# Two-layer streaming encoder: the sample streams as nine units inside the pair pipeline of both attention layers, and the first tile's bias loaded ahead of the band

## The reference, cut to what matters

```
# layer 0: 16 heads in 2 key/value groups; keys = 16 meta + 128 cached + 16 own = 160
keys = concatenate([km, ck, k]);  vals = concatenate([vm, cv, v])
s = einsum(q, keys) * D ** -0.5 + bias          # bias from the distance of query and key
p = sink_softmax(s, sinks)                      # the sink is one more term of the sum
o = einsum(p, vals)
# layer 1: 16 heads, 1 key/value group; keys = 256 cached + 16 own, of which each query
# keeps the 68 with the best index scores, + 16 meta that are always kept = 288
```

## Time and profile before

| | us |
|---|---|
| three runs | 3144.76, 3155.63, 3156.03 |
| median | 3155.63 |
| profiled execution | 3155.8 |
| its span, first to last instruction | 3154.0 |
| stream pipeline and what is ahead of it, layer 0 | 173.5 to 261.2 |
| prompt pipeline, layer 0 | 261.2 to 436.9 |
| stream pipeline, layer 1 | 1740 to 1841 |
| prompt pipeline, layer 1 | 1841 to 2149.3 |

### The profile page before, as it was taken

How to read it: one execution, slowest core, us unless ns; L and a number is a source line. 1 busy time by engine, 2 the same in 40 slices (tenths; PEclk the granted TensorE clock), 3 DMA queues, 4 the chain that set the end, 5 groups by cost and what they waited for, 6 DMA issues and landing times.

```text
span 3154.0 us, 47535 instructions
## 1 busy us (share of the span) xinstructions
PE 2985.0 (95%) x18119; PEld 2784.0 (88%) x18119; DVE 1550.6 (49%) x2822; ACT 708.0 (22%) x1424; POOL 879.8 (28%) x825
## 2 busy tenths in 40 slices
PE   7969999999999999998895999999999999999998
PEld 6957889999999999986585777779899999999997
DVE  5125633644444444454498357552454444444445
ACT  3025631100000000023366236652100000000001
POOL 3212333222222222222033136322322222222221
PEclk9966999999999999999997559999999999999998
DMA  3521001111111111113011100002111111111111
GB/s 116 81 73 33 2 15 41 34 41 40 40 40 40 40 40 40 40 33 116 9 43 39 49 13 2 2 2 83 39 41 40 40 40 40 40 46 41 40 33 70
DMA packets 182948, 130.26 MB, mean 41 GB/s; under 512 B 32241, under 2 KB 172977, under 8 KB 182598
## 3 DMA queue, kind: packets, MB, share of 16 engines
q1 hardware_dynamic: 182818, 128.52, 14.3%
HBM read 112.80 MB, written 15.16 MB: 41 GB/s over the span
## 4 chain that ended last, share of the span: by engine, by line
PE 87%; DVE 6%; issue 4%; SPq 1%; ACT 1%; DMA 0%; DVEq 0%; POOL 0%; POOLq 0%; ACTq 0%
PE ps_gemm L1406 33%; PE ps_gemm L1422 18%; PE ps_gemm L1372 16%; PE ps_tr L1493 4%; PE ps_out L1513 2%; PE ps_tr L1489 2%; PE ps_far L1790 1%; PE ps_far L1623 1%; PE ps_near L1513 1%; PE ps_far L1810 1%; PE ps_out L1510 1%; DVE scm L2340 1%; PE ps_out L1830 1%; PE ps_near L1510 1%; DVE xl L2114 1%
## 5 line engine op out<-in xcount | busy, mean ns | idle before, releaser
L692 DVE TENSOR_TENSOR h<-h,ps_gemm 128x1170 f32<-128x1170 f32 x192 | 263.7, 1374 | 407.4 <-PE ps_gemm L1422 231.8
L1406 PE MATMUL ps_gemm<-xh,w_hi 128*128 128x390 f32 x1920 | 448.1, 341 | 0.0
L1406 PE MATMUL ps_gemm<-xh,w_lo 128*128 128x390 f32 x1920 | 448.1, 342 | 0.0
L1406 PE MATMUL ps_gemm<-xl,w_hi 128*128 128x390 f32 x1920 | 446.0, 340 | 0.0
L1224 POOL CAST w_hi<-w_raw 128x1024 fp32r<-128x1024 f32 x120 | 124.9, 1041 | 1130.9 <-PE ps_gemm L1406 625.6
L1406 PEld LDWEIGHTS ps_gemm<-xh,w_hi 128*128 128x128 f32 x1920 | 352.5, 189 | 0.0
L1406 PEld LDWEIGHTS ps_gemm<-xl,w_hi 128*128 128x128 f32 x1920 | 349.4, 189 | 0.0
L1406 PEld LDWEIGHTS ps_gemm<-xh,w_lo 128*128 128x128 f32 x1920 | 349.1, 189 | 0.0
L1227 POOL TENSOR_TENSOR w_lo<-w_raw,w_hi 128x1024 fp32r<-128x1024 f32 x120 | 287.4, 2395 | 17.4
L1372 PE MATMUL ps_gemm<-xl,w_hi 128*128 128x390 f32 (+1 forms) x1152 | 271.6, 344 | 0.0
L1422 PE MATMUL ps_gemm<-gu_hi,w_hi 128*128 128x390 f32 x1056 | 247.6, 343 | 0.9 <-DVE h L692 0.9
(11 more groups left out here) (378 smaller groups left out, 4609.9 us busy)
## 6 DMA issues: line engine op xcount, KB each, us to landing
w_raw<-in_w_gate SPq DMA_DIRECT2D x44, 512.0 KB, 3.8
w_raw<-in_w_up SPq DMA_DIRECT2D x44, 512.0 KB, 3.8
w_raw<-in_w_down SPq DMA_DIRECT2D x44, 512.0 KB, 3.2
w_raw<-in_w_in_b SPq DMA_DIRECT2D x13, 512.0 KB, 4.0
w_raw<-in_w_qkv_a SPq DMA_DIRECT2D x10, 512.0 KB, 4.0
residual_park<-h SPq DMA_DIRECT2D x1, 4680.0 KB, 13.7
h<-residual_park SPq DMA_DIRECT2D x8, 585.0 KB, 7.5
out<-yt SPq DMA_DIRECT2D x9, 512.0 KB
```

Of the source, the lines that this page charges most:

```text
L692: dve.tensor_tensor(c3(h[:, m, :]), c3(h[:, m, :]), pse(j), ALU.add).then_inc(evac[j % 2], 1)
L1406: mm = pe.matmul(ps[j % 2][:, m_, 0:CH], w[:, k, :], x[:, k, m_ * CH:(m_ + 1) * CH], start=(k == 0 and w is wh and x is XH), stop=(k == KT ...
```

## The change

One list of 73 units, `UNITS`, now serves both layers: the 64 pairs and 9 stream units, of which one follows each sixth pair from pair 11 on (b = -1 is the meta rows, then streams 0 to 7). The pipeline `attention` is gone. A stream unit is both halves of a unit at once: its 128 rows are (head pair, query), its halves r = 0, 1 are the heads of a pair, so all 16 heads go through in one unit. Keys are brought into both halves by products with the identity (`keys_a`, `keys_b`) two steps ahead, and the values' products write the output already transposed. The mask of a stream comes to 128 rows by 8 small DMAs (`mask_s`) and POOL adds it to the bias (`comb_s`). The slots of transposed groups are 4 in both layers. The first tile's bias is loaded first, then `vbd`, then the band; the band's masking is put behind step 4 of the pipeline. In layer 1 the mask steps are two behind each of the first 24 steps. `to_rows` is gone.

```diff
+        UNITS = []
+        for n in range(QT * HEADS // 2):
+            UNITS.append({"n": n, "t": n // 8, "pr": n % 8, "b": None})
+            if n >= 11 and (n - 11) % 6 == 0:
+                UNITS.append({"n": None, "t": None, "pr": None, "b": (n - 11) // 6 - 1})
...
-            if layer == 0:
-                k = j % 6
-                return x12["pta"][:, k, :] if k < 3 else x4["pta_v"][:, k - 3, :] if k < 5 else x4["pta_s"][:]
-            k = (j - NV[1]) % 7
-            return hreg["ptb_a"][:, k, :] if k < 2 else hreg["ptb_b"][:, k - 2, :] if k < 5 else x4["ptb_x"][:, k - 5, :]
+            k = (v - V0[layer]) % 4
+            if layer == 0:
+                return x4["pta_v"][:, k, :] if k < 2 else x12["pta_x"][:] if k == 2 else rreg["pta_r"][:]
+            return hreg["ptb_a"][:, k, :] if k < 2 else hreg["ptb_h"][:] if k == 2 else x4["ptb_x"][:]
...
+            def keys_a(g):
+                j, b = g["j"], UNITS[g["keys"]]["b"]
+                pe.wait_ge(sa_in[b % 2], 48 * (b // 2 + 1))
+                if j >= 2:
+                    pe.wait_ge(p_ev[j % 2], j // 2)
                 for kv in range(KV_A):
+                    d = slice(HD * kv, HD * (kv + 1))
+                    for src, rows, c in ((x12["sa_k"], P, 0), (x12["sa_kc"], 32, P)):
+                        for p in range(2):
+                            mm = pe.matmul(tb[j % 2][HD * p:HD * (p + 1), 160 * kv + c:160 * kv + c + rows],
+                                           src[0:rows, b % 2, d], ident[0:rows, 0:rows], start=True, stop=True)
+                mm.then_inc(p_tr, 1)
...
+            def stream_scores_a(i, b, o):
+                pe.wait_ge(p_q, b + 2)
+                if b >= 0:
+                    j = KEY_GROUP[0][i]["j"]
+                    pe.wait_ge(p_ev[j % 2], j // 2 + 1)
+                for p in range(2):
+                    r = slice(HD * p, HD * (p + 1))
+                    for g in range(KV_A):
+                        c = slice(HD * g, HD * (g + 1))
+                        k = x4["kts_a"][r, g, :] if b >= 0 else kt_a(g)[r, 0:META]
+                        mm = pe.matmul(far[p][c, o:o + unit_width(0, i)], x12["qs_a"][r, c], k, start=True, stop=True)
+                mm.then_inc(p_sc, 1)
...
+                for p in range(2):
+                    r = slice(HD * p, HD * (p + 1))
+                    lhs, x = hreg["qs_b"][r, :], far[p]
...
+                    pe.matmul(x[:, o:o + PAST], lhs, hreg["kts_b"][r, 0:PAST], start=True, stop=True)
+                    pe.matmul(x[:, o + PAST:o + PAST + DEC_SEQ], lhs, x4["kt2"][r, scols(b)], start=True, stop=True)
+                    mm = pe.matmul(x[:, o + 272:o + 288], lhs, hreg["kts_b"][r, PAST:PAST + META], start=True, stop=True)
...
+            def mask_between(n):
+
+                for s in (2 * n, 2 * n + 1):
+                    c, k = divmod(s, MASK_STEPS)
+                    if c < 6:
+                        mask_step(c, k, first_mask + MASK_STEPS * c)
```

More of the change, by code:

```diff
@@ L388, in units_a @@
[L388 to L397, removed]
-                    else:
-                        u["blocks"] = [(1, 32), (33, P)]
-                        u["w"] = 160
-                        if g == 0 and b + 1 < DEC_BATCH:
-                            u["pre"] = [b + 1]
-                    us.append(u)
-            return us
@@ L550, in build, with score_counts @@
+        RED, FREE = reductions()
+        def score_counts():
+            got, count = [[], []], 0
+            for layer in range(2):
+                for i in range(NU):
+                    t = UNITS[i]["t"]
+                    two = layer and t is not None and 3 <= t < 6
+                    got[layer].append((count + 1, count + (2 if two else 1)))
+                    count = got[layer][-1][1]
+            return got
+        SC = score_counts()
         parked = sem("residual_parked")
@@ L1476, in prompt @@
[L1476 removed]
+            def prompt(layer, scores, keys, values, meta_values):
                 def transposes(g):
[L1479 removed]
+                    j, i = g["j"], g["u"]
                     if g["first"]:
[L1481 removed]
+                        pe.wait_ge(p_exp, 2 * (NU * layer + i) + 2)
                     if j >= 2:
                         pe.wait_ge(p_ev[j % 2], j // 2)
[L1484 to L1485 removed]
+                    x = x_of(layer, i)
+                    for k, b in enumerate(g["blocks"]):
@@ L1528, in prompt @@
-                for g in VG[layer][-2:]:
-                    products(g)
+                    gs = AT[layer][n]
+                    if gs and gs[0]["keys"] is not None:
+                        keys(gs[0])
+                        gs = gs[1:]
+                    for k in range(0, len(gs), 2):
+                        for g in gs[k:k + 2]:
+                            transposes(g)
+                        for g in gs[k:k + 2]:
+                            if g["v"] - 2 >= V0[layer]:
+                                products(BY_V[g["v"] - 2])
@@ L1531, in _ @@
+                for v in range(V_END[layer] - 2, V_END[layer]):
+                    products(BY_V[v])
             pe.wait_ge(ident_in, 16)
```

1115 lines of the change are left out of this document (462 added, 653 removed).

## The result

| | before | changed |
|---|---|---|
| median of the runs | 3155.83 us (4 runs) | 3060.4 us (4 runs, 3051.24 to 3061.28) |
| profiled execution | 3155.8 us, span 3154.0 | 3051.24 us, span 3049.5 |
| ratio | 1 | 0.9697, 95% interval 0.9666 to 0.9727 |

The time fell by 95 us by the medians and by 104.5 by the two traces.

The account below looks back on a forecast made before the run. PE was taken to bound the prompt pipelines, with streams costing nearly 190 us at half clock. Layer 0's terms gave -42.6 and layer 1's -56.7, together -99.3 from 3155.8: forecast 3056 us, range 3038 to 3092.

Parts of the forecast that it names:

- Start of layer 0: Layer 0's first prompt reduction at 182.5 in place of 260.45, no stream work ahead: 78.0 us earlier (69 to 80).
- Start of layer 1: Layer 1's first prompt reduction at 1740.3 in place of 1842.42, with the band already landed: 102.1 us earlier (99 to 103).
- The streams: Stream units on PE in both pipelines: 4.0 us per stream, 1.4 for the meta unit, 33.4 us per layer (27 to 46).
- The test named in the prediction: In the pipelines, a gap of about 4.0 us between a stream's scores and those of the next pair.
- The slots: Four slots for transposed groups in place of 6 and 7: costs nothing (0 to +5 us).
- The mask steps: Layer 1, two per step behind the first 24 steps: DVE needs longer than PE in steps 12 to 23, +12 us (0 to +20).
- the sign named for it: In layer 1's steps 12 to 23, PE idle for some 12 us with DVE as releaser.
- The clock: Layer 0's pipeline: the clock could rise later than 23 us after the prompt's start, +2 us (0 to 9).
- Rival A: Low clock in layer 1's steps 12 to 23, perhaps around later streams: +20 to +40 us, 3076 to 3096; chance 0.16.
- B: Both pipelines: each stream unit costs its upper bound, waits adding 1.6 us to each of 16: 3082 us; chance 0.12.
- C: Pipeline starts: layer 0 starts at 191 and layer 1 waits for its band, +9 + 3, 3068 us; chance 0.07.
- D: Both mixed pipelines: the clock never rises, set back by streams and waits on DVE; about 3380 us; chance 0.03.

Follow-up runs that it names:

- the test: Changed kernel plus, at its end, five forms of VectorE mask steps with GpSimd idle, then beside GpSimd's additions; 3144.8 us, 93 us of it these additions to the kernel.
- the control: The changed kernel run again unaltered in a later batch; median 3057.8 us, single runs 3054.6 to 3062.6.
- the trimmed version: Changed kernel with TensorE's idle time ahead of both pipelines filled, by fewer products than in the first fill, and mask steps four per three units; 3029.9 us.
- the best version: The trimmed version with five and three filling products in layer 0 in place of three and one; 3022.0 us, ratio 0.959 to the kernel before.
- the version with both the overrun and the spread steps: Changed kernel with the first, longer fill of TensorE's idle time, which ran past the first reduction in layer 1, and mask steps over 36 units; 3038.7 us.

## Why the prediction was right, and which of its terms were not

The forecast, 3056 us, is 4 us under the median and 5 over the profiled execution, and the mechanism is the one forecast: the streams leave their half-clock stretches, both pipelines start 78 and 105 us earlier, and the streams come back at full clock. That it came within 5 us of the trace owes something to luck. Split by the run without streams, the terms were off by -4.0 (streams, layer 0), +1.7 (clock, layer 0), +1.9 (streams, layer 1), -1.7 (mask steps and clock, layer 1), +0.3 and -3.2 (the two starts) us, which sum to -5. By its own steps:

**Start of layer 0: right.** -78.0 was said, -77.75 measured, with the landing at 181.6 where 182.0 was said.

**Start of layer 1: 3 us short.** -102.1 against -105.3. From the memset to the reduction it was 1.6 us, not 1.9. The rest: the memset itself stood 1297.2 us behind the first product of layer 0's projection, 3.0 less than before. These three lie ahead of the end of layer 1's last projection (1262.4 us behind that product, against 1265.8 before), not in the search. Their cause is open.

**The streams: right in sum, with the wrong split.** 33.4 per layer was said, 66.8 in all; without the streams but with the leading tokens' unit the total fell by 62.7, where 64 would be due. A stream costs 3.5 us in layer 0 and 4.2 in layer 1, not 4.0 in each. The timeline of layer 0 shows the period directly, from the scores of one stream to those of the next; the scores of the next pair follow a stream's after 2.35 us:

```profile
237.20 0.50 PE L1569 MATMUL ps_far<-kts_a,qs_a 64*64 64x160 f32 x8
...
239.55 0.70 PE L1554 MATMUL ps_far<-kt,q 64*128 64x256 f32 x4
...
256.79 0.50 PE L1569 MATMUL ps_far<-kts_a,qs_a 64*64 64x160 f32 x8
```

From stream to stream it is 19.59 us, six pairs of 2.68 and 3.5 for the stream. By starts in the same timeline, these are keys 1.21 us (1.07 was said), scores 0.43 (0.75), transposes 0.59 (0.56), the inverse 0.27 (0.27), values 0.84 (1.06) and 0.17 by which the transposes behind the keys take longer, where 0.3 was put for waiting. The scores and the values were priced too high. The test named in the prediction, a gap of 4.0 us between a stream's scores and the next pair's, was put badly: a stream's work is spread over four steps, and the price is only in the period.

**The slots: nothing speaks against it.** The run with three shows at most some 3 us for a slot less; the step from six and seven to four was not run by itself.

**The mask steps: right in size, and the reason incomplete.** +12 was said; the pipeline of layer 1 without streams is 11.7 us longer than before (with 1.4 for the leading tokens' unit in it), and spreading the steps gives back 11.6. But the sign named for it, PE idle for some 12 us with DVE as releaser, did not come: in the 62 us window PE is idle for 8.1 us, of which 4.2 end with DVE and 3.7 with ACT's copies. The rest goes with the fall of the clock. DVE was taken to be busy with the steps for the time they took before. In fact the same ten groups sum to 46.3 us (1692.3 to 1800) against 39.4, which had one step less. I take GpSimd's additions beside them for the cause. The comparison over 768 elements took 1.73 us in the changed kernel with GpSimd adding, 0.87 in the kernel before, and in the test 0.62 alone and 1.33 beside GpSimd:

```profile
1735.75 1.73 DVE L2324 TENSOR_SCALAR eq<-scm,small 128x768 bf16<-128x768 f32 x1
```

**The clock: wrong reading, small error.** In layer 0 it rose 28.8 us behind the first reduction, not 23, one to two steps late, as allowed for; in the control another 9 us later. Without streams and the leading tokens' unit layer 0's pipeline is 3.7 us longer than before, where +2 stood. Rival A came true in small: the clock did fall once in steps 12 to 23, for 7 us, in the wait on DVE shown above; in the control it fell there for 10 us and again near 1780. What the prediction missed is that in layer 1 it rose after 31.6 us, where before it took 42, which hid that loss.

The Trainium skill, TensorE: Matmul & The Clock Gate, section "What's actually happening", says that TensorE is held at the lower clock by default and that activity releases it. In this case's traces the granted clock stays at 0.50 for 28.8 us in which PE shows as busy for 28.09 (the windows above; the earlier trace rows has the same in the kernel before); with the idle time ahead of the pipeline filled, the same steps run at 1.00. So busy time in the profile alone does not tell which level is granted, and no run here shows what does.

**Profile and median.** By the median the gain is 9 us less than by the trace. The control's trace, at 3054.6 us, has 3.3 us of that in layer 0's pipeline, where the clock rose later. The remainder I put down to the same cause, since the time of single runs falls as their granted clock rises; it is not shown, for only the profiled runs show where the clock is low.

**Rivals.** B (5.6 us a stream) is refuted by the period and by the run without streams, C (191 and a late band) by the first reduction at 182.70 and the band's issue at 1655.93, and D by the clock row. The low end of the range, 3038, was said to be half of the small bounds' 25 us; half would be 3043.5. Nothing here hangs on it.

## What to carry to other kernels

When work at half clock is moved into a pipeline that runs at full clock, price it by the pipeline's own instructions at full clock and check the period over several units; here 4.0 us a stream was said and 3.5 and 4.2 came. Work whose deadline is far off, such as the mask steps, should be paced to its last deadline and not packed into the first steps: one number in the loop gave 12 us. Both pipelines here follow idle time and ran their first steps at half clock; filling that time gave 6 to 10 us in layer 0 and 6 to 8 in layer 1. Fill with as many products as fit and no more, counted from a measured one: with two mask steps per unit, 6 us of gain in layer 1 became 7 us of loss by an overrun.

## What the hardware showed that was not expected

- In these pipelines of short products with many weight loads the clock stayed at 0.50 for 21 to 38 us behind the first reduction though PE shows as busy nearly all the time; once it is up, the same steps mostly keep it at 1.00. It fell at one wait of 2.1 to 2.6 us in each of seven traces, and in the trimmed version behind a wait of 1.83 us; waits of up to 1.1 us in the four traces with spread mask steps left layer 1's pipeline at 1.00.
- The time at which it rises differs by 9 us between two executions of one kernel (28.8 and 37.7 us behind the first reduction). Five runs of the best version, whose trace has no stretch at 0.50 in either pipeline, lie within 1 us; but the five of the version with both the overrun and the spread steps, whose trace has none either, lie 8 us apart, with granted clocks of 0.984 to 0.988.
- A VectorE operation with its inputs in SBUF, beside a GpSimd that adds without a pause, took 0.65 to 0.77 us longer in all five forms tried, whatever its own length (0.62 to 1.76 us); GpSimd's addition took 1.65 us in place of 1.09.
- Three bias loads of 1.2 MB took 6.8 and 6.9 us to issue behind 2 MB of band, and 2.2 us ahead of it.
